# Gated delta rule in a two-block kernel: two value heads inverted in one matrix, block transposes on VectorE

## The reference, cut to what matters

```python
decay = jnp.exp(jnp.where(incl, gc[..., :, None] - gc[..., None, :], -jnp.inf))
kk = jnp.einsum("bhncd,bhnjd->bhncj", k, k)
m = jnp.where(strict, beta[..., :, None] * kk * decay, 0.0) + jnp.eye(C, dtype=f32)
rhs = jnp.concatenate([v * beta[..., None], k * (beta * jnp.exp(gc))[..., None]], axis=-1)
sol = lax.linalg.triangular_solve(m, rhs, left_side=True, lower=True, unit_diagonal=True)
```

## Time and profile before

| what | value |
|---|---|
| median of three runs | 3418.48 us (3417.89 to 3418.68) |
| profiled execution: span from first to last instruction | 3413.1 us |
| profiled execution: its own time | not listed beside its span |
| TensorE (PE) busy | 3254.4 us, 95% |
| VectorE (DVE) busy | 1421.6 us, 42% |
| ScalarE (ACT) busy | 910.3 us, 27% |
| GpSimd (POOL) busy | 1704.4 us, 50% |
| mean granted TensorE clock | 0.989 of full speed |
| DMA | 306.52 MB, mean 90 GB/s |

### The profile page before, as it was taken

One profiled execution on the slowest core, in us unless ns is written; L12 is line 12 of the kernel. 1 busy time (PEld: TensorE's weight loads), 2 busy tenths in 40 slices (PEclk: granted clock), 3 DMA queues, 4 the chain that ended last, 5 costly groups with the idle time before them and its releaser, 6 DMA issues.

```text
span 3413.1 us, 46693 instructions
## 1 busy us (share of the span) xinstructions
PE 3254.4 (95%) x16752; PEld 2712.9 (79%) x16752; DVE 1421.6 (42%) x1929; ACT 910.3 (27%) x1411; POOL 1704.4 (50%) x1748
## 2 busy tenths in 40 slices
PE   8999989999999999999999999999998999999996
PEld 7877878888888888888788887787777878778685
DVE  6722234333433343334331314333356565631723
ACT  5411133333333333333320102111113333310411
POOL 0255634433443344334326777765664555556684
PEclk9999999999999999999999999999999999999998
DMA  6322212211221122112224223222223222223222
GB/s 238 124 85 94 82 55 74 74 55 55 74 74 55 55 74 74 55 55 86 98 69 172 99 91 143 99 92 86 95 97 120 68 88 69 94 91 122 77 96 86
DMA packets 53530, 306.52 MB, mean 90 GB/s; under 512 B 5044, under 2 KB 7220, under 8 KB 21716
## 3 DMA queue, kind: packets, MB, share of 16 engines
q1 hardware_dynamic: 34528, 248.53, 21.2%
q10 hardware_dynamic: 18932, 57.00, 4.5%
HBM read 284.74 MB, written 20.77 MB: 90 GB/s over the span
## 4 chain that ended last, share of the span: by engine, by line
PE 80%; DVE 12%; ACT 5%; issue 2%; DMA 1%; ACTq 0%; DVEq 0%; SPq 0%
PE gemm_ps L436 19%; PE gemm_ps L438 19%; PE gemm_ps L437 19%; DVE arena L878 9%; PE bankC L580 4%; PE bankA L571 3%; ACT arena L1579 2%; PE gemm_ps L795 2%; DVE a_lo L878 2%; PE gemm_ps L797 2%; PE gemm_ps L796 2%; PE bankA L751 2%; PE bankB L587 1%; ACT a_hi L1579 1%; PE bankA L593 1%
## 5 line engine op out<-in xcount | busy, mean ns | idle before, releaser
L436 PE MATMUL gemm_ps<-a_hi,w_hi 128*128 128x512 f32 (+1 forms) x3472 | 1390.8, 401 | 15.4 <-DVE a_lo L878 13.4
L412 POOL CAST w_hi<-w_raw 128x512 fp32r<-128x512 f32 x872 | 547.2, 670 | 1661.9 <-issue 1504.2
L438 PE MATMUL gemm_ps<-a_hi,w_lo 128*128 128x512 f32 (+1 forms) x3472 | 1331.9, 384 | 0.0
L437 PE MATMUL gemm_ps<-a_lo,w_hi 128*128 128x512 f32 (+1 forms) x3472 | 1329.9, 383 | 0.0
L404 POOL TENSOR_TENSOR w_lo<-w_raw,w_hi 128x512 fp32r<-128x512 f32 x872 | 1161.0, 1363 | 4.2
L436 PEld LDWEIGHTS gemm_ps<-a_hi,w_hi 128*128 128x128 f32 x3472 | 657.5, 189 | 145.9 <-DVE a_lo L878 16.3
L438 PEld LDWEIGHTS gemm_ps<-a_hi,w_lo 128*128 128x128 f32 x3472 | 655.4, 189 | 131.2
L437 PEld LDWEIGHTS gemm_ps<-a_lo,w_hi 128*128 128x128 f32 x3472 | 657.5, 189 | 119.2 <-issue 9.0
L878 DVE TENSOR_TENSOR arena<-gemm_ps,arena 128x512 f32<-128x512 f32 (+3 forms) x161 | 107.1, 665 | 615.5 <-PE gemm_ps L438 496.3
L1579 ACT ACTIVATE arena<-arena 128x512 f32<-128x512 f32 (+5 forms) x350 | 214.6, 613 | 397.9 <-DVE arena L878 383.0
L878 DVE RECIPROCAL arena<-arena 128x512 f32<-128x512 f32 (+2 forms) x70 | 172.8, 2468 | 321.7 <-ACT arena L1579 319.7
(11 more groups left out here) (161 smaller groups left out, 2516.6 us busy)
## 6 DMA issues: line engine op xcount, KB each, us to landing
w_raw<-w_stream SPq DMA_DIRECT2D x236, 1024.0 KB, 4.9
y_scratch<-arena ACTq DMA_DIRECT2D x20, 512.0 KB, 3.4
arena<-y_scratch ACTq DMA_DIRECT2D x13, 512.0 KB, 4.3
arena<-gc_scratch ACTq DMA_DIRECT2D x12, 512.0 KB, 3.6
arena<-x_t ACTq DMA_DIRECT2D x2, 2048.0 KB, 10.1
arena<-y_scratch ACTq DMA_DIRECT2D x1, 4096.0 KB, 24.1
x_scratch<-arena ACTq DMA_DIRECT2D x1, 4096.0 KB, 15.7
y_out<-arena ACTq DMA_DIRECT2D x4, 1024.0 KB, 3.9
```

Source lines behind the costliest of these rows:

```text
L412: pool.tensor_copy(part(w_hi, w, q), part(w_raw, w, q)).then_inc(pool_step, 1)
L436: pe.matmul(o, hi, a_hi[:, k, 0:width], start=(k == 0), stop=False)
L437: pe.matmul(o, hi, a_lo[:, k, 0:width], start=False, stop=False)
L438: last = pe.matmul(o, lo, a_hi[:, k, 0:width], start=False, stop=(k == KT - 1))
```

## The change: what it does

Only the mixing of the delta rule changes. The matrices of value head 0 and value head 1 are put into one 128x128 matrix per chunk, one in each triangle (`pair_n`); `inv_b` (the first half of `XT`) and `inv_a` (the second) hold the two growing inverses in the same way, one the transposed counterpart of the other. A level then has four products in `half` and four in `whole`, for both value heads together, instead of eight and eight.

At levels 0 to 4 every block lies within 32 rows and columns. There VectorE's `transpose`, which transposes 32x32 blocks, takes the place of TensorE's: one from `inv_b` to bankC, from which a masked copy takes rows (`level_rows`, mask by row from the constant `rows`), and one from `inv_a` to bankB, from which ScalarE copies the inner columns (`inner`) in the next level. At levels 5 and 6 TensorE transposes (`turn`, `flip`, and four transposes behind the last `whole`). Step `transposed` is gone; `dT`, `kd`, `ke` and small factors are made within levels 1 to 4. Value head 1 now carries other scale factors (`v_scale`, `u_scale`, `ke_scale`, `neg_k`). Weights of the steps change, their sum stays 96. The core of the diff, with its indentation cut:

```diff
-DN_STEPS = ([("natural", 10), ("values", 8), ("transposed", 6)]
-+ [(s, l, a, w) for l in range(1, LEVELS - 1)
-   for s, a, w in (("half", 0, 0), ("half", 1, 0), ("whole", 0, 0), ("whole", 1, 1), ("turn", 0, 1),
-                   ("turn", 1, 1))]
-+ [(s, LEVELS - 1, a, w) for s, a, w in (("half", 0, 2), ("half", 1, 0), ("whole", 0, 1), ("whole", 1, 0))]
-+ [("solved", 6)]
+DN_STEPS = ([("natural", 12), ("values", 12)]
++ [(s, l, w) for l in range(1, LEVELS - 2) for s, w in (("half", 1), ("whole", 4))]
++ [("half", LEVELS - 2, 1), ("whole", LEVELS - 2, 1), ("turn", 3)]
++ [("half", LEVELS - 1, 1), ("whole", LEVELS - 1, 2), ("flip", 2), ("solved", 4)]
 + [(s, n, g) for n in range(NB) for s, g in (("rest", 2), ("output", 3))]
-+ [("head_out", 28)])
++ [("head_out", 18)])
...
-E, dT, NmT, X, XT, T1, kd, vn = (units(o_ + 1024 * k) for k in range(8))
-ke, U = E, X
+E, dT, Nm, U, XT, T1, kd, vn = (units(o_ + 1024 * k) for k in range(8))
+ke = E
+pair_n, turned0 = Nm[:, 0, :, :], Nm[:, 1, :, :]
+inv_b, inv_a = XT[:, 0, :, :], XT[:, 1, :, :]
+half_t = T1[:, 0, :, :]
...
+def inner(x, l):
 
 h = 1 << l
-return x.rearrange("p (b t) -> p b t", t=2 * h)[:, :, h * second:h * second + h]
-
-def level_mask(mask, l, second):
-
-h = 1 << l
-m = half_columns(mask[:, l, :], l, second)
-return m[:, None, :, :].to_broadcast([P, NB, P // (2 * h), h])
-
-def level_blocks(x, l, second):
-
-h = 1 << l
-return x.rearrange("p (n b t) -> p n b t", n=NB, t=2 * h)[:, :, :, h * second:h * second + h]
+return x.rearrange("p (b t) -> p b t", t=4 * h)[:, :, h:3 * h]
...
-    elif step[0] == "transposed":
-        pe.wait_ge(s["x_ready"], j + 1)
-        pe.wait_ge(s["vn_sbuf"], j + 1)
-        for a in range(2):
-            for n in range(NB):
-                last = pe.transpose(quad(bankC)[:, a, n, :], XT[:, a, n, :], ident)
-        last.then_inc(s["nT"], 1)
     elif step[0] == "half":
-        l, a = step[1:3]
-        if l > 1:
-            pe.wait_ge(s["t1_sbuf"], product_count(j, l - 1, a) + 2)
-        else:
-            pe.wait_ge(s["nT_sbuf"], j + 1)
-            pe.wait_ge(s["pm_ready"], j + 1)
+        l = step[1]
+        pe.wait_ge(s["inv_ready"], 2 * level_count(j, l) - 1)
         for n in range(NB):
-            last = pe.matmul(quad(bankA)[:, a, n, :], NmT[:, a, n, :], X[:, a, n, :],
+            last = pe.matmul(quad(bankA)[:, 0, n, :], pair_n[:, n, :], inv_a[:, n, :],
                              start=True, stop=True)
         last.then_inc(s["t1"], 1)
     elif step[0] == "whole":
-        l, a = step[1:3]
-        pe.wait_ge(s["t1_sbuf"], product_count(j, l, a))
+        l = step[1]
+        pe.wait_ge(s["t1_sbuf"], level_count(j, l))
+        pe.wait_ge(s["inv_ready"], 2 * level_count(j, l))
         if l == 1:
-            pe.wait_ge(s["kd_ready"], j + 1)
+            pe.wait_ge(s["vn_sbuf"], j + 1)
         for n in range(NB):
-            last = pe.matmul(quad(bankC)[:, a, n, :], T1[:, a, n, :], XT[:, a, n, :],
+            last = pe.matmul(quad(bankC)[:, 0, n, :], half_t[:, n, :], inv_b[:, n, :],
                              start=True, stop=True)
         last.then_inc(s["dd"], 1)
-    elif step[0] == "turn":
-        l, a = step[1:3]
-        pe.wait_ge(s["lvl"], level_count(j, l, a))
+        if l == LEVELS - 1:
+            for n in range(NB):
+                pe.transpose(quad(bankB)[:, 1, n, :], inv_a[:, n, :], ident)
+    elif step[0] in ("turn", "flip"):
+        pe.wait_ge(s["lvl"], 3 * j + (1 if step[0] == "turn" else 2))
         for n in range(NB):
-            last = pe.transpose(quad(bankB)[:, a, n, :], XT[:, a, n, :], ident)
-        last.then_inc(s["dd"], 1)
+            last = pe.transpose(quad(bankC)[:, 1, n, :], inv_b[:, n, :], ident)
+        last.then_inc(s["turned"], 1)
     elif step[0] == "solved":
         for a in range(2):
-            pe.wait_ge(s["lvl"], level_count(j, LEVELS - 1, a))
+            pe.wait_ge(*((s["xt1"], j + 1) if a else (s["lvl"], 3 * j + 3)))
             for n in range(NB):
                 last = pe.matmul(quad(bankA)[:, a, n, :], XT[:, a, n, :], vn[:, a, n, :],
                                  start=True, stop=True)
         last.then_inc(s["solved"], 1)
+        pe.wait_ge(s["kd_ready"], j + 1)
...
+def level_rows(l, turned, j):
+
+    copy_after(v.copy_predicated, chunks(XT, 1), rows[:, l:l + 1].bitcast(U32).to_broadcast([P, T]), turned,
+               sem=s["inv_ready"], value=2 * level_count(j, l + 1) - 1)
+
 def dn_mix(step, j, g=None):
     flat = "p a n t -> p (a n) t"
     pair_ = [NB, 2]
     if step[0] == "natural":
         op(v.tensor_copy, XT[:, :, :, :].rearrange(flat), ident[:, None, :].to_broadcast([P, 8, P]))
+        v.wait_ge(s["expd"], 2 * j + 2)
+        op(v.tensor_tensor, qd, cv[:, 0:1, :].to_broadcast([P, 2, T]), gcb, ALU.mult)
         v.wait_ge(s["k_root"], j + 1)
         op(v.reciprocal, kinv, kroot)
-        kinv2 = kinv[:, :, None].to_broadcast([P, *pair_])
+        op(v.reciprocal, kinv_ps, kroot)
+        kinv2 = kinv_ps[:, :, None].to_broadcast([P, *pair_])
         op(v.tensor_tensor, neg_br, cb[:, :, 1, :], kinv2, ALU.mult)
         op(v.tensor_tensor, neg_c, neg_br, kinv2, ALU.mult)
+        op(v.tensor_scalar, v_scale, neg_br[:, :, 1], -1.0, None, ALU.mult)
         v.wait_ge(s["pair"], j + 1)
-        v.wait_ge(s["expd"], 2 * j + 1)
-        for a in range(2):
+        for a, to in ((1, pair_n), (0, quad(bankA)[:, 0, :, :])):
             for n in range(NB):
-                op(v.scalar_tensor_tensor, NmT[:, a, n, :], bankA[:, 0, n * P:n * P + P],
+                op(v.scalar_tensor_tensor, to[:, n, :], bankA[:, 0, n * P:n * P + P],
                    neg_c[:, n, a:a + 1], E[:, a, n, :], ALU.mult, ALU.mult)
-        copy_after(v.copy_predicated, XT[:, :, :, :].rearrange(flat),
-                   lowT[:, 0:1, :].to_broadcast([P, 8, P]), NmT[:, :, :, :].rearrange(flat),
-                   sem=s["x_ready"], value=j + 1)
+        copy_after(v.copy_predicated, pair_n, incl[:, None, :].bitcast(U32).to_broadcast([P, NB, P]),
+                   quad(bankA)[:, 0, :, :], sem=s["pm_ready"], value=j + 1)
+        copy_after(v.copy_predicated, inv_b, both_ways[:, 0:1, :].to_broadcast([P, NB, P]), pair_n)
+        op(v.transpose, chunks(Nm, 1), chunks(XT, 0))
+        level_rows(0, chunks(Nm, 1), j)
+        op(v.tensor_copy, inner(chunks(XT, 0), 0).rearrange("p (n b) t -> p n b t", n=NB),
+           inner(ident, 0)[:, None, :, :].to_broadcast([P, NB, P // 4, 2]),
+           sem=s["inv_ready"], value=2 * level_count(j, 1))
+        op(v.tensor_tensor, kd_scale, cb[:, :, 2, :], kinv2, ALU.mult)
+        op(v.tensor_tensor, ke_ps, cb[:, :, 3, 1], kinv_ps, ALU.mult)
+        op(v.tensor_tensor, ke_scale[:, :, 1], ke_ps, v_scale, ALU.mult)
+        op(v.transpose, bankB[:, 1, :], chunks(XT, 1))
         for n in range(NB):
             op(v.scalar_tensor_tensor, dTm[:, n, :], bankA[:, 1, n * P:n * P + P], kinv[:, n:n + 1],
                incl, ALU.mult, ALU.mult)
-        v.wait_ge(s["expd"], 2 * j + 2)
-        op(v.tensor_tensor, qd, cv[:, 0:1, :].to_broadcast([P, 2, T]), gcb, ALU.mult,
-           sem=s["pm_ready"], value=j + 1)
-    elif step[0] == "transposed":
-        op(v.tensor_tensor, kd_scale, cb[:, :, 2, :], kinv[:, :, None].to_broadcast([P, *pair_]), ALU.mult)
-        op(v.tensor_tensor, dT[:, :, :, :], E[:, :, :, :], both(dTm), ALU.mult)
-        op(v.tensor_tensor, kd[:, :, :, :], both(by_chunk(bankB[:, 0, :])), by_row(kd_scale), ALU.mult)
-        op(v.tensor_tensor, ke[:, :, :, :], both(by_chunk(bankB[:, 0, :])), by_row(cb[:, :, 3, :]), ALU.mult,
-           sem=s["kd_ready"], value=j + 1)
-        op(v.tensor_scalar, pos_br, neg_br, -1.0, None, ALU.mult)
     elif step[0] == "whole":
-        l, a = step[1:3]
-        v.wait_ge(s["dd"], product_count(j, l, a))
+        l = step[1]
+        v.wait_ge(s["dd"], level_count(j, l))
+        late = l >= LEVELS - 2
+        copy_after(v.copy_predicated, inv_b, both_ways[:, l:l + 1, :].to_broadcast([P, NB, P]),
+                   quad(bankC)[:, 0, :, :], sem=s["lvl"] if late else None, value=3 * j + l - LEVELS + 3)
+        if late:
+            return
+        op(v.transpose, bankC[:, 1, :], chunks(XT, 0))
+        level_rows(l, bankC[:, 1, :], j)
         if l == 1:
-            changed = (XT[:, a, :, :], lowT[:, l:l + 1, :].to_broadcast([P, NB, P]), quad(bankC)[:, a, :, :])
+            op(v.tensor_tensor, dT[:, :, :, :], E[:, :, :, :], both(dTm), ALU.mult)
+        elif l == 2:
+            op(v.tensor_copy, ke_scale[:, :, 0], cb[:, :, 3, 0])
+            op(v.tensor_scalar, u_scale[:, :, 0], neg_br[:, :, 0], -1.0, None, ALU.mult)
+            op(v.tensor_copy, u_scale[:, :, 1], kroot)
+            op(v.tensor_scalar, neg_k, kroot, -1.0, None, ALU.mult)
+        elif l == 3:
+            op(v.tensor_tensor, kd[:, :, :, :], both(by_chunk(bankB[:, 0, :])), by_row(kd_scale), ALU.mult)
         else:
-            changed = (level_blocks(chunks(XT, a), l, 1), level_mask(lowT, l, 1),
```

(73 more changed lines are left out.)

11 lines of the change are left out of this document (4 added, 7 removed).

## The result

| | median | runs |
|---|---|---|
| before | 3418.18 us | 3413.67 to 3418.68 (4) |
| changed | 3284.12 us | 3278.72 to 3288.24 (4) |
| forecast | 3217.5 us | range 3186 to 3262 |

The ratio is 0.9611 [0.9597, 0.9625]: faster by 134 us, where 201 were forecast. The time lies 22 us above the range. The profiled execution has a span of 3286.4 us (3413.1 before), 127 us less.

The account below looks back on a forecast made before the run. TensorE, busy 95% of the span, was taken as the bound. Eleven heads at 16.9 us (186) plus 15 in the last gave 201 us off 3418.5: 3217.5 us, range 3186 to 3262.

Parts of the forecast that it names:

- TensorE's work removed: Per head, 48 of 96 level products (10.75 us) and 36 net transposes (3.15 us) would leave TensorE.
- The block transpose: VectorE's transpose in the levels, seen in no row, was taken at 0.73 us like the masked copy.
- Rivals 2 and 3: VectorE transposes take 1.5 us (3256 us, chance 0.08), or run at the reciprocal's pace, 3.35 us (3432 us, chance 0.03).
- being of one tensor input like line 1059's, I take 1.4: Level 2's four tiny VectorE operations, possibly 0.7 to 4.4 us, were put at 1.4 us in all.
- the wait charged at 1.5: Tiny operations and taps delay the masked copy before level 3's end: 1.5 us a looped head (0.9 to 4.6).
- Rival 1: Port contention with GpSimd makes the four tiny operations cost 4.4 us: 3251 us, chance 0.15.
- A cost put at nothing: Old levels: slow clock behind a wait, about 1 us; a fall in the new levels was only named as lessening the gain.
- A normal level: Levels 1 to 4, from one `half` to the next: 5.50 us each, four 22.0 us.
- The head I summed against: Old levels of head 4, 44.37 us from first `half` to `solved`, were the base for a looped head's gain.
- The last head: No taps there; levels gain 12.9 us, `transposed` 0.8, a wait shrinks by about 1: together 15 us.
- Nearly without a wait, and with no slack either: Levels 1 to 4: chain through VectorE allows the next `half` at 5.50 us, TensorE alone needs 5.42.
- rival 3: Transposes at the reciprocal's pace: rows-to-rows distances 10.2, 11.7, 9.7 and 8.1 us, summed as 39.9; chance 0.03.

Follow-up runs that it names:

- e1: Changed kernel with the four tiny scale-factor operations moved from level 2 to level 1, behind its second block transpose: 3238.85 us.
- e4: Changed kernel with other weights: `values` 12 to 8 parts, five instead of four parts behind each `whole` in levels 1 to 4: 3227.63 us.
- e2: Changed kernel with the first block transpose of levels 1 to 4 issued twice: 3336.60 us.
- e3: Changed kernel with the last head's tile 0 of the output projection added before VectorE's share of the second `whole`, not behind part 31: 3271.35 us.
- e7: The changed kernel run again, unedited, beside the other variants: 3281.88 us.
- e6: Changed kernel with TensorE instead of VectorE's first block transpose turning the inverse in levels 1 to 4, products still shared: 3284.47 us.
- e8: Changed kernel with TensorE turning the inverse in levels 1 to 4 and the four tiny operations moved to level 1: 3267.51 us.

## Why the prediction was wrong, point by point

The forecast had 16.9 us of gain in each looped head and 15 in the last; 67 us of the 201 did not come. No single step lost them. Each of the following has its size from the stretches of the profiled executions.

- **TensorE's work removed: right.** 13.9 us a head, 167 in twelve; the 135 us less of busy time and the 22 of slow clock leave about 10, and fp32 blocks that wait show longer, as below. All stretches of heads 3 and 4 outside the levels came out to 0.1 us.
- **The block transpose: right.** 0.73 us taken, 0.727 measured over 108 of them into PSUM, 0.711 into SBUF. The Trainium skill states one element per cycle and lane (Vector Engine (DVE) Microarchitecture Reference, section 3.8). The trace is in keeping with it, since a masked copy over the same 512 columns takes 0.73 too; no run has another width, so the rate by itself is not shown. Rivals 2 and 3 are out.
- **The step that failed: "being of one tensor input like line 1059's, I take 1.4" for the four tiny operations.** From the start of the first to the end of the last they took 2.5 us in head 4 and 3.8 in head 7, and the wait charged at 1.5 was 2.4 to 3.6, 2.84 on average: 13 us in ten heads. Line 1059's median was a bad witness: eleven of its twelve ran while GpSimd was idle, and the one that started under a subtraction took 1.26, which was the case that applied. The runs have the four at 0.17 us beside an idle GpSimd (e1, e4), 0.45 to 0.65 when held by its casts and 1.2 to 1.3 by its subtractions. The Trainium skill (SBUF — State Buffer, "Who interferes with whom") had said that such copies can contend; the trace agrees (0.17 against 1.28 us). Rival 1 was the right mechanism; its 4.4 us were reached in e2 (4.2), not in the changed kernel.
- **A cost put at nothing.** I had the slow clock behind a wait in view, yet charged nothing for it behind the new one. Waits of 3.5 to 3.6 us brought it in all 11 cases in heads 2 to 11 of the changed kernel, e3 and e7, those of 2.4 in 10 of 19, mostly 1.2 us each: 10 us in ten heads. Waits of 0.36 us (e1) and 1.6 us (e6) never did in heads 2 to 11.
- **A normal level: nearly, but it counts.** 5.68 us for 5.50. Without the wait and the slow clock the six levels take 36.0 us (head 3: 38.4 - 2.4), where the sum has 34.6: 13 us in ten heads. The chain is longer than I added it up, by 0.2 to 0.3 us a level. A part of that: an fp32 block that had to wait for its semaphore takes 0.91 us to the next part, not 0.81 (762.67 and 768.42 above), and so `whole` starts 1.85 behind `half`. In e4, where `half` doesn't wait, it is 0.81 in all six levels of head 4.
- **The head I summed against was not a typical one.** Head 4's levels took 44.37 us; the mean of heads 2 to 11 is 43.25, since only heads 4, 7 and 10 had the slow clock. 1.1 us too much gain a head, 11 us in ten.
- **The last head: 15 us forecast, 4 had.** "The last head has no taps" was true; that VectorE frees tile 0 at the same place, behind all of level 2, I left out. 5.6 us of wait and the slow clock behind it. Its old levels took 38.5 us, not the 39.3 that I took.
- **The first head** became 11.7 us shorter (123.45 to 111.78), not 16.9: 5 us.
- 13 + 10 + 13 + 11 + 11 + 5 = 63 of the 67 us missing. The profiled execution of the changed kernel, the slowest of its four, lost 11 us more outside the heads. 9 of them lie between the last `head_out` and the end, where the change has no part: 1621.3 us, and 1611.9 before without the ten parts that now come earlier. The mean granted clock there was 0.982, and 0.987 before, which is worth 8.5 us. Over all ten profiled executions of the changed kernel and its variants this stretch took 1611.8 to 1621.3 us.
- **"Nearly without a wait, and with no slack either"** was true, and should have set the range: a chain without slack passes each delay on, in full. With the four tiny operations elsewhere the time falls into the range (e1, 3238.85 us).
- Two sums in the prediction are off by 0.2 us and change nothing: 2.2 + 0.8 + 24 parts is 19.3, not 19.5, and rival 3's four distances add up to 39.7, not 39.9.

Of the change's two ideas, sharing the products, which also halves the transposes, carries most. With TensorE turning the inverse in levels 1 to 4 (e8) the gain is 149 us; VectorE's first block transpose of these levels brings 29 more (e1). What the second one brings was not measured. In the changed kernel as it was, nearly all of the 29 was lost again: e6, without the first block transposes, has looped heads only 0.6 us longer.

## What to carry to other kernels

When work moves from a full engine to a queue with room, look at what stands in that queue ahead of each result that the full engine waits for, tile-freeing operations included; a mean busy share of 48% says nothing of it. Operations on a few elements are not free: place them where GpSimd is idle. Products of 8 elements with one of their two inputs in PSUM kept their 0.16 us under GpSimd's subtractions; for one-input operations that was not tried. If a dependent chain just fits, give it one part more of cover before anything else: e4 is two numbers and brought 56 us.
